# Time mix on one core: decay's low-rank product over rows and difference, key's scale on VectorE, bonus behind the first scores

## What is computed

```
h  = rms_norm(x, norm_g[0, 0])
xx = pad(h)[:-1] - h                                  # the token before, less this one
xr, xw, xk, xv, xa, xg = [h + xx * mu[i] for i in range(6)]
r, k, v = xr @ w_rkv[0], xk @ w_rkv[1], xv @ w_rkv[2]
w = -softplus(-(w_decay0 + tanh(xw @ w_decay1) @ w_decay2)) - 0.5
a = sigmoid(a0 + (xa @ a1) @ a2)
g = sigmoid(xg @ g1) @ g2
kk = k * k_k, scaled to length 1 in each head
k  = k * (1 + (a - 1) * k_a)
S_t = S_{t-1} * exp(-exp(w_t)) + (S_{t-1} @ -kk_t) (kk_t * a_t) + v_t k_t ;   y_t = S_t @ r_t
y  = group_norm(y) + sum(r * k * r_k) * v             # the last term is the bonus
out = (y * g) @ w_o
```

## Time and profile before

| | |
|---|---|
| runs, us | 1520.93 median of 3 (1519.63 to 1522.9) |
| profiled execution, us | 1519.45, with a span of 1517.7 |
| PE busy | 1413.9 us, 93% of the span |
| DVE, ACT busy | 61% and 50% |
| chain that ended last | PE 84%, DVE 9%, ACT 5%, issue 2%, DMA 1% |
| mean granted clock of PE | 0.958 |

### The profile page before, as it was taken

The page is one execution under the profiler, slowest core; times in us unless marked ns, Lnnn a source line. Parts: engine busy times, 40 slices in busy tenths (PEclk is TensorE's granted clock), DMA queues, the critical chain, the costliest instruction groups (busy, mean ns, idle before and its releaser), DMA issues.

```text
span 1517.7 us, 27277 instructions
## 1 busy us (share of the span) xinstructions
PE 1413.9 (93%) x11109; PEld 1266.0 (83%) x11109; DVE 928.3 (61%) x1355; ACT 754.1 (50%) x1166; POOL 43.9 (3%) x79
## 2 busy tenths in 40 slices
PE   5988988789999898899998999999999998899998
PEld 4867988379999787799997898799997787789997
DVE  6847332666676757666767465755557566565554
ACT  4562321165555755655557464544445464454443
POOL 5000000010000000000000000010001000000000
PEclk9998988599999999999999999999999999999999
DMA  7420001455555440555554554556654543245550
GB/s 221 135 103 1 4 3 44 166 155 193 188 172 194 142 168 25 186 203 193 167 193 147 186 185 148 164 174 191 193 187 146 178 165 102 84 159 180 190 191 29
DMA packets 135073, 222.25 MB, mean 146 GB/s; under 512 B 6137, under 2 KB 105697, under 8 KB 134720
## 3 DMA queue, kind: packets, MB, share of 16 engines
q1 hardware_dynamic: 132688, 214.19, 43.4%
q0 software_dynamic: 2144, 6.61, 1.4%
q10 hardware_dynamic: 144, 0.06, 0.0%
HBM read 219.77 MB, written 1.05 MB: 145 GB/s over the span
## 4 chain that ended last, share of the span: by engine, by line
PE 84%; DVE 9%; ACT 5%; issue 2%; DMA 1%; SPq 0%; DVEq 0%; ACTq 0%
PE ps L477 81%; DVE ulo L463 1%; ACT uhi L455 1%; DVE scratch L1799 1%; PE ps L771 1%; DVE x_sb L1773 1%; DMA raw<-in_w_rkv 1%; PE ps L1082 0%; DVE scratch L2087 0%; DVE xn_lo L1761 0%; DVE xs L1749 0%; ACT scratch L1310 0%; DVE x_sb L1779 0%; PE ps L918 0%; ACT xn_hi L1341 0%
## 5 line engine op out<-in xcount | busy, mean ns | idle before, releaser
L463 DVE TENSOR_TENSOR ulo<-raw,uhi 128x1024 fp32r<-128x1024 f32 x400 | 488.3, 1224 | 383.4 <-ACT uhi L455 383.1
L455 ACT ACTIVATE uhi<-raw 128x1024 fp32r<-128x1024 f32 x400 | 422.7, 1059 | 442.8 <-PE ps L477 437.5
L477 PE MATMUL ps<-xn_hi,uhi 128*128 128x256 f32 x1472 | 418.0, 284 | 6.7 <-DVE xn_lo L1815 2.6
L477 PE MATMUL ps<-xn_lo,uhi 128*128 128x256 f32 x1472 | 416.5, 283 | 0.0
L477 PE MATMUL ps<-xn_hi,ulo 128*128 128x256 f32 x1472 | 416.4, 283 | 0.0
L477 PEld LDWEIGHTS ps<-xn_hi,uhi 128*128 128x128 f32 x1472 | 282.3, 192 | 10.5 <-issue 4.0
L477 PEld LDWEIGHTS ps<-xn_lo,uhi 128*128 128x128 f32 x1472 | 282.4, 192 | 1.7
L477 PEld LDWEIGHTS ps<-xn_hi,ulo 128*128 128x128 f32 x1472 | 282.3, 192 | 0.0
L477 PE MATMUL ps<-uhi,xm_hi 128*128 128x512 f32 x512 | 201.3, 393 | 1.8 <-DVE xm_lo L2035 1.1
L477 PE MATMUL ps<-ulo,xm_hi 128*128 128x512 f32 x512 | 200.6, 392 | 0.0
L477 PE MATMUL ps<-uhi,xm_lo 128*128 128x512 f32 x512 | 159.9, 391 | 0.0
(11 more groups left out here) (273 smaller groups left out, 1331.2 us busy)
## 6 DMA issues: line engine op xcount, KB each, us to landing
raw<-in_mlp_w SPq DMA_DIRECT2D x64, 1024.0 KB, 5.3
raw<-in_w_up SPq DMA_DIRECT2D x44, 1024.0 KB, 5.1
raw<-in_w_down SPq DMA_DIRECT2D x22, 1024.0 KB, 4.9
raw<-in_gmlp_w_in SPq DMA_DIRECT2D x16, 1024.0 KB, 5.4
raw<-in_fox_w_in SPq DMA_DIRECT2D x16, 1024.0 KB, 5.3
raw<-in_w_rkv SPq DMA_DIRECT2D x12, 1024.0 KB, 6.2
raw<-in_gmlp_w_out SPq DMA_DIRECT2D x8, 1024.0 KB, 4.8
raw<-in_w_o_rwkv SPq DMA_DIRECT2D x4, 1024.0 KB, 5.9
```

The costliest lines, as they stand in the source:

```text
L455: nc.scalar.activation(ring_unit(uhi, m, n), raw_unit(n, j), ACT.Copy).then_inc(hi_done, 1)
L463: nc.vector.tensor_tensor(ring_unit(ulo, m, n), raw_unit(n, j), ring_unit(uhi, m, n).bitcast(F32), ALU.subtract).then_inc(lo_done, 1)
L477: return nc.tensor.matmul(o, l, r, start=start, stop=stop, skip_group_check=True)
```

## The change

- `weight_stream`: the first slot of `r` is loaded ahead of `L1A`, which becomes the second slot.
- ACT's and DVE's `upto(2)` at the start go: ACT copies `hT` first, then writes a second, scaled copy of `w_decay1` behind `L1A` (rows times `mu[1]`, 8 instructions of 64 columns), then splits units 0 and 1. DVE subtracts at once, piece by piece (`xx_done`), and splits unit 0 only after the mix for r, unit 1 in the middle of `xn_lo`.
- The decay's product is no longer over a mix: PE multiplies `w_decay1` with `hT` and the scaled copy with the difference `xx`, 8 products each into one bank, so 24 products in place of 16. `mix(1)` is gone.
- DVE's order during `r` is: unit 2, the small vectors, mix 2, unit 3, mix 5, unit 4, `xm_lo`, unit 5, mix 3, units 6 and 7. ACT rounds the mix for k after quarter 0 of `r` and not after quarter 1.
- `key_scale` moves from ACT to DVE (8 `tensor_scalar` with two per-partition scalars), behind unit 11.
- The bonus's sums stand behind the two `sb` stages and go to bank 0; ACT empties them there, behind the split of units 24 and 25.

```diff
-    phase("lora1", [("L1A",)])
-    phase("r", [u(rkv[0], 256 * q) for q in range(4)])
+    r = [u(rkv[0], 256 * q) for q in range(4)]
+    phase("r", [r[0], ("L1A",), *r[1:]])
...
-    stages = [("kn", q, 0) for q in range(4)] + [("bonus", 0, 0)] + prepare(0)
+    first = prepare(0)
+    stages = [("kn", q, 0) for q in range(4)] + first[:2] + [("bonus", 0, 0)] + first[2:]
...
# tensor
-            for j in range(2):
-                for k in range(NF):
-                    pe.wait_ge(lmix_done, NF * j + k + 1)
-                    last = mm(bank(j, T)[64 * j:64 * j + 64, :], l1a[:, 128 * k + 64 * j:128 * k + 64 * j + 64],
-                              mixes[j][:, k, :], k == 0, k == NF - 1)
-                last.then_inc(lora_ps, 1)
+            for k in range(NF):
...
+                pe.wait_ge(hT_done, k + 1)
+                mm(bank(4, T)[0:64, :], l1a[:, 128 * k:128 * k + 64], hT[:, k, 1:T + 1], k == 0, False)
+            for k in range(NF):
+                if k == 0:
+                    pe.wait_ge(lw_done, 1)
+                if k % 2 == 0:
+                    pe.wait_ge(xx_done, k // 2 + 1)
+                last = mm(bank(4, T)[0:64, :], l1a[:, 1024 + 64 * k:1088 + 64 * k], f3(S(S_X))[:, k, :], False,
+                          k == NF - 1)
+            last.then_inc(lora_ps, 1)
+            for k in range(NF):
+                pe.wait_ge(lmix_done, k + 1)
+                last = mm(bank(1, T)[64:128, :], l1a[:, 128 * k + 64:128 * k + 128], f3(S(S_MB))[:, k, :], k == 0,
+                          k == NF - 1)
+            last.then_inc(lora_ps, 1)
...
+            pe.wait_ge(lora_done, 1)
             proj("r", 0, xn_hi, xn_lo, first_split=0, split_done=rlo_done)
...
# scalar
-            upto(2)
...
+            l1a = raw[:, special[0] % RAW, :]
+            act.wait_ge(landed[special[0] % RAW], landed_at(special[0]))
+            for k in range(NF):
+                last = A_(l1a[:, 1024 + 64 * k:1088 + 64 * k], l1a[:, 128 * k:128 * k + 64], ACT.Copy,
+                          scale=col(V_MU + 8 + k))
+            last.then_inc(lw_done, 1)
+            upto(2)
...
-            proj("r", f3(S(S_R)), after={1: lambda: mixhi(1, S_MA, xm_hi)})
+            proj("r", f3(S(S_R)), after={0: lambda: mixhi(1, S_MA, xm_hi)})
...
-                 after={0: decays, 1: decays_back, 2: key_scale})
+                 after={0: decays, 1: decays_back})
...
# vector
+            dve.wait_ge(proj_done, 12)
+            for f in range(NF):
+                last = TS(f3(S(S_W))[:, f, :], f3(S(S_A))[:, f, :], col(V_KA + f), omka[:, f:f + 1], ALU.mult, ALU.add)
+            last.then_inc(ka_done, 1)
             upto(18)
```

More of the change, by code:

```diff
@@ L859, in _ @@
             d_gemm(pe, "v", xn_hi, xn_lo, before=before_v)
[L861 to L867, removed]
             pe.wait_ge(ops_done, 1)
-            pe.wait_ge(v_done, 2)
             def wait_moved(stage):
@@ L890, in core @@
                         wait_moved((r, i, g))
-                if name in ("sb", "sk"):
+                if name == "bonus":
+                    pe.wait_ge(v_done, 2)
+                    rk = f3(S(S_W))
+                    for tok in range(NT):
+                        for f in range(NF):
+                            last = mm(bank(0, 2, 16 * tok + 2 * f), rk[:, f, P * tok:P * tok + P], rks[:, f, :], True,
+                                      True)
+                elif name in ("sb", "sk"):
                     for j in range(4):
@@ L959, in core @@
                 last.then_inc(core_ps, 1)
-            for st in stages[5:]:
+            for st in stages[4:]:
                 core(*st)
@@ L1382, in _ @@
                        scale=col(V_NORM + 2 * b + f)).then_inc(hT_done, 1)
+            l1a = raw[:, special[0] % RAW, :]
[5 more added lines that the diff above has]
+            upto(2)
             act.wait_ge(lora_ps, 1)
-            A_(lh[0:64, :], bank(0, T)[0:64, :], ACT.Tanh).then_inc(lora_done, 1)
+            A_(lh[0:64, :], bank(4, T)[0:64, :], ACT.Tanh).then_inc(lora_done, 1)
             act.wait_ge(lora_ps, 2)
@@ L1422, in decays_back @@
                 act.sem_inc(ee_done, 1)
-            def key_scale():
-                act.wait_ge(proj_done, 12)
-                for f in range(NF):
-                    last = A_(f3(S(S_W))[:, f, :], f3(S(S_A))[:, f, :], ACT.Identity, scale=col(V_KA + f),
-                              bias=omka[:, f:f + 1])
-                last.then_inc(ka_done, 1)
             proj("k", f3(S(S_K)), squares=f3(S(S_H)), square_cols=V_KK,
-                 after={0: decays, 1: decays_back, 2: key_scale})
+                 after={0: decays, 1: decays_back})
             act.wait_ge(ksum_done, 1)
@@ L1438, in _ @@
                 A_(xs[:, tok, :], acc(tok), ACT.Copy).then_inc(v_done, 1)
-            act.wait_ge(core_ps, 5)
-            A_(sm[:, 16:48], bank(4, 32), ACT.Copy).then_inc(moved[0], 1)
             upto(26)
@@ L1444, in _ @@
             for k, (name, i, g) in enumerate(stages):
-                if name not in (*core_act, "rv", "tok", "u"):
+                if name not in (*core_act, "rv", "tok", "u", "bonus"):
                     continue
                 act.wait_ge(core_ps, k + 1)
+                if name == "bonus":
+                    A_(sm[:, 16:48], bank(0, 32), ACT.Copy).then_inc(bon_done, 1)
                 for q, b in enumerate(ring_bank[k]):
@@ L1794, in _ @@
                           hT[:, 2 * b:2 * b + 2, 1:T + 1], ALU.subtract)
-            step(last)
+                last.then_inc(xx_done, 1)
+            dve.wait_ge(xx_done, 4)
             def mix(k, dst, done=None):
@@ L1817, in _ @@
                 if f == 3:
-                    upto(3)
+                    upto(2)
+            upto(3)
             dve.wait_ge(vec_ps, 2)
             vectors([1, 2, 3, 4], 2)
+            mix(2, S_MA)
             upto(4)
-            dve.wait_ge(lora_ps, 1)
-            mix(2, S_MA)
-            upto(6)
-            mixlo(1, S_MA, xm_hi, xm_lo)
-            upto(7)
             dve.wait_ge(lora_ps, 2)
             mix(5, S_MB)
-            upto(8)
+            upto(5)
+            mixlo(1, S_MA, xm_hi, xm_lo)
+            upto(6)
             dve.wait_ge(mixlo_done, 1)
             mix(3, S_MA)
+            upto(8)
             dve.wait_ge(vec_done, 2)
@@ L1855, in _ @@
             dve.wait_ge(dd_done, 1)
-            TT(S(S_MB), S(S_MA), S(S_W), ALU.subtract).then_inc(dd_done, 1)
+            step(TT(S(S_MB), S(S_MA), S(S_W), ALU.subtract))
+            dve.sem_inc(dd_done, 1)
+            upto(12)
+            dve.wait_ge(proj_done, 12)
+            for f in range(NF):
+                last = TS(f3(S(S_W))[:, f, :], f3(S(S_A))[:, f, :], col(V_KA + f), omka[:, f:f + 1], ALU.mult, ALU.add)
+            last.then_inc(ka_done, 1)
             upto(18)
```

17 lines of the change are left out of this document (10 added, 7 removed).

## The result

The changed kernel took 1506.09 us (median of 4 runs, 1504.22 to 1511.5), the kernel before 1521.91 on the same chip (1519.63 to 1523.7). The ratio is 0.9906, with a 95% interval of 0.9883 to 0.993.

A forecast was written before the change was run, and what follows sets the result against it. PE's own work bounds most of the execution, so only its waits in the first 150 us can go: 4.9 + 1.9 + 1.6 = 8.4 off 1519.45, predicted median 1512.5 us (forecast 1510.5 to 1515, range 1507.5 to 1517.7).

The forecast's parts named there:

- time lost in `r`: During `r`: DVE's splits behind larger pieces lose 0.1, 1.5, 0.5 and 1.5 us, leaving 4.9 of the opening's 5.75.
- idle before `head_sums`: End of `k`: without `key_scale` on ACT, PE's idle of 4.21 us falls to 2.3, a gain of 1.9.
- wait before `ad`: End of `v`: ACT splits units 24 and 25 earlier, masks and `ad` follow, a gain of 1.6 us.
- sum at `ad`: Gains of 4.9 in opening and `r`, 1.9 at end of `k`, 1.6 at end of `v`: 8.4 us.
- The opening: Before unit 0: DVE begins `xn_lo` at 23.4 and not 29.25, PE finishes unit 0 at 28.25: gain 5.75 us.
- The key's scale: On DVE it takes 2.2 to 3.3 us, hidden by 6.07 us of DVE idle before units 13 and 14: cost 0.
- The bonus: End of `v`: its 3.63 us end at 142.8, inside PE's idle stretch before `ad` at 145.5, so covered.
- The profiled execution took 1519.45, so 1511.05: Whole kernel: 8.4 us off the profiled execution; the median lies 1.5 above it, giving 1512.5.
- PE late in the opening: Rival: `L1A` lands 2 us later and the clock falls, costing 3.2 more; together 5.2, 1517.7 us; chance 0.14.
- `L1A` last: Rival: `L1A` finishes with the other slots of `r`, near 22.6; 4.9 us slower, 1525.8; chance 0.05.
- Clock gains as well: Rival: shorter idle keeps PE's clock up, 1.7 us more at `head_sums`, up to 1.4 from `ad`: 1509.4; chance 0.15.
- The change gives nothing: Rival: splits during `r` held up by more than one mix each; four more 1.5 us stalls, 1518.5; chance 0.03.

The follow-up runs named there:

- the mix as an operand: Changed kernel with the decay's 16 products over the mix again, `mix(1)` back on DVE, no scaled weights, split order kept: 1512.37 us, ratio 0.9955 to the kernel before.
- the splits moved: Changed kernel with each of DVE's splits of units 3 to 7 during `r` ahead of the large piece before it: 1505.8 us, ratio 0.9908 to the kernel before.
- the masks first: Changed kernel with DVE's split of units 24 and 25 behind the masks of the first score stage: 1504.44 us, ratio 0.9896 to the kernel before.
- key's scale alone: Kernel before with only the key's scale moved to VectorE (DVE): 1518.73 us, ratio 0.9984.
- bonus alone: Kernel before with only the bonus moved behind the score stages: 1518.11 us, ratio 0.9985.
- opening alone: Kernel before with only load order, product over rows and difference, and split order during `r` changed: 1515.03 us, ratio 0.9968.
- changed, second: The changed kernel unaltered, compared again with the kernel before: 1510.61 us, ratio 0.9939.
- changed, `L1A` first: Changed kernel with `L1A` loaded ahead of unit 0's slot again: 1508.27 us, ratio 0.9924 to the kernel before.
- changed, third: The changed kernel unaltered, compared a third time with the kernel before: 1509.82 us, ratio 0.9921.
- the one with filler: Changed kernel with ten needless float32 products on PE in its idle stretch before `head_sums`, output unchanged: 1504.11 us, ratio 0.9887 to the kernel before.
- last quarter first: Changed kernel with ACT emptying and squaring the last quarter of `k` ahead of unit 18's high part: 1506.18 us, ratio 0.9893 to the kernel before.
- all together: Changed kernel with DVE's splits one place earlier during `r`, masks ahead of units 24 and 25, last quarter of `k` emptied first: 1499.35 us, ratio 0.9847 to before.

## Why the prediction was right in its parts and short in its sum

Up to `ad`, step by step, with the first profile of the changed kernel against the earlier trace rows:

| step | predicted | measured |
|---|---|---|
| unit 3's high part (34.00 before) | 28.25, gain 5.75 | 27.94, gain 6.06 |
| PE's waits in `r`, units 3 to 6 | 0.1, 1.5, 0.5, 1.5 | none, 1.13, 0.20, 1.18 |
| time lost in `r`, units 3 to 7 (2.9 before) | 3.7 | 51.37 - 27.94 - 7 x 2.88 = 3.3 |
| end of `r` | gain 4.9 | 56.86 - 51.20 = 5.66 |
| idle before `head_sums` | 2.3 | 2.42; its start 100.60 - 93.16 = 7.44, so 1.8 on top |
| wait before `ad` | 2.7, gain 1.6 | 1.82; 147.13 - 137.98 = 9.15, so 1.8 more than the 7.34 at the first score |
| sum at `ad` | 8.4 | 9.15 |

**The opening held.** Its mechanism is shown by the two kernels that take it apart: the mix as an operand costs 3.2, the rest are the splits. Of the gain of 6.06 some 0.4 is none of the change's: PE's transposes began at 8.18 and not at 8.63, since the first small load landed earlier. Two terms were too small. ACT's copy of 64 columns I took as 0.17 between bounds of 0.08 and 0.33; it is 2.06 / 8 = 0.26 each. The weights were ready at 15.61, PE's first eight products through at 15.50, and that cost PE 0.16, but the opening nothing: ACT had its first `xn_hi` by 22.8 and DVE only came to `xn_lo` at 23.21, so it was DVE that was last and not ACT, as I had it. There the mix was too small, 7.68 / 16 = 0.48 and not 0.447. My 0.447 was a mean over 24 mixes, and one of them is held up in either kernel. In the changed one it is this, with POOL's instruction that stands beside it:

```profile
20.29 1.20 POOL L634 TENSOR_SCALAR_AFFINE_SELECT xs<-xs 16x1024 f32<-16x1024 f32 x1
20.38 1.38 DVE L1811 SCALAR_TENSOR_TENSOR scratch<-scratch,vec 128x256 f32<-128x256 f32 x1
```

In the kernel before the same pair stands at 21.53 and 21.62, with the same durations. The other mixes take 0.47 to 0.56 and follow each other every 0.39 to 0.49. No run moved POOL's instruction, so that it is the cause is not tested; but a cost of 0.9 us that comes once doesn't shrink with the number of mixes.

**The time lost in `r` was put too high by 0.4.** It is counted from split to split on ACT: unit 3's high part to the split behind the last unit, less seven units of 2.88. Before it was 2.9, the prediction has 3.7 (1.5 + 0.5 + 1.5 + 0.1, and by a slip the 0.1 once more), and the changed kernel has 3.3: unit 3 was in time, and units 4, 5 and 6 waited less than I had. The three idle rows of PE add up to 2.5 only. In a run the passes start every 0.12 and are recorded 0.28 long, and the idle time is counted from the end of that 0.28; behind a wait the second pass starts 0.22 after the first. So each wait costs some 0.25 more than its row says. The cause is the one named: with the splits moved 0.3 is left of the 3.3.

**The key's scale was hidden**, as predicted. It took 2.67 / 8 = 0.33 each, between the bounds of 0.27 and 0.41 and not at the lower one, and DVE still idles 4.63 us behind it:

```profile
72.13 2.67 DVE L1873 TENSOR_SCALAR scratch<-scratch,vec,sm 128x256 f32<-128x256 f32 x8
74.72 1.21 DVE L467 TENSOR_TENSOR ulo<-raw,uhi 128x1024 fp32r<-128x1024 f32 x1
80.56 2.36 DVE L467 TENSOR_TENSOR ulo<-raw,uhi 128x1024 fp32r<-128x1024 f32 x2 [4.63 <-ACT uhi L459]
```

**The bonus was covered**, and what was late next were units 24 and 25, as the step says; the kernel with the masks first shows it.

**Where the sum failed: "The profiled execution took 1519.45, so 1511.05".** That step carries the 8.4 from `ad` to the end, as if all behind it took the same time. It doesn't, from one execution to the next. The table has the start of `ad`, the first instruction of the group norm behind the recurrence (a DVE reduction), the time between them, and from there to the end of the span; the code behind `ad` is the same in all of them.

| profile of | `ad` | group norm | between | from there on |
|---|---|---|---|---|
| before | 147.13 | 273.51 | 126.4 | 1244.2 |
| key's scale alone | 147.67 | 274.17 | 126.5 | 1242.7 |
| bonus alone | 146.52 | 272.52 | 126.0 | 1243.8 |
| opening alone | 141.66 | 268.25 | 126.6 | 1241.7 |
| changed, first | 137.98 | 259.32 | 121.3 | 1243.2 |
| changed, second | 138.24 | 260.64 | 122.4 | 1242.5 |
| changed, `L1A` first | 139.77 | 263.32 | 123.5 | 1243.3 |
| changed, third | 139.71 | 265.77 | 126.1 | 1242.8 |

In the first comparison 5.0 of the 15.2 us of span lie between `ad` and the group norm, and 1.0 behind that. The 126.1 of the third profile and the 121.3 of the first belong to the same kernel, so they can be laid side by side. Ninety us behind `ad`, at the same products, PE's timeline reads, first profile and then third:

```profile
225.75 7.57 PE L481 MATMUL ps<-raw 64*64 64x64 f32 x252 [0.29 <-issue]
```

```profile
229.99 10.19 PE L481 MATMUL ps<-raw 64*64 64x64 f32 x295 [2.09 <-issue]
```

and the stretches of 3 us around them, first profile and then third:

```profile
226.00:229.00 3.00, 3.00 (x110) 3.00 (x106) 0.76 (x2) 0.98 (x2) 0.00 (x0) 1.00 0.12 45
229.00:232.00 3.00, 3.00 (x110) 3.00 (x108) 0.00 (x0) 2.22 (x5) 0.00 (x0) 1.00 0.03 5
```

```profile
228.00:231.00 3.00, 1.01 (x19) 1.00 (x20) 1.21 (x2) 0.00 (x0) 0.00 (x0) 0.78 0.16 60
231.00:234.00 3.00, 3.00 (x76) 3.00 (x74) 0.00 (x0) 0.60 (x1) 0.00 (x0) 0.65 0.02 5
```

PE stands for 2.09 us and waits for nothing that the profile shows, and the clock falls behind it, to 0.65 over a stretch, so that 3 us of it hold 76 products and not 110. The profiles of before, of the opening, the key's scale and the bonus alone have this stop too (1.92, 2.33, 2.20 and 2.87 us); the first and second of the changed kernel and the one with `L1A` first have at most 0.44 us of it. From the place of the stop to the group norm the third profile takes 37.9 us and the first 33.9, so stop and clock are 4.0 of the 4.7 between them. Before it was 35.9: against the first profile 2.0 of the 5.0 lie there, and the other 3.0 ahead of the stop, where the clock differs as well (0.50 from 195 to 201 before, 0.72 from 186 to 192 in the first profile, both 48 us behind `ad`).

The stop happens while three loads of 512 KB on POOL's queue fill the DMA engines. An instruction block moves among them. These are the us in which it starts, of the first profile (223 to 224) and then of the third (227 to 228), with queue and kind, packets, MB, share of the 16 DMA engines:

```profile
q0 software_dynamic: 73, 0.26, 82.9%
q8 instruction: 1, 0.02, 6.0%
```

```profile
q0 software_dynamic: 101, 0.37, 96.8%
q8 instruction: 1, 0.02, 6.0%
```

I read the stop as PE's instructions coming late behind the loads. Thirteen of the fourteen profiles have idle time of this kind at this point, from 0.20 to 3.72 us, and they bear the reading out in two ways. First the place: in twelve of them, whatever the kernel, 3114 to 3116 passes of PE since the start of the program precede it, and in the one with filler 3242, 127 more; in the first profile two more such rows, of 0.44 and 0.19 us, stand 252 and 378 passes behind the first. So it hangs on how many instructions PE has had, and not on what they compute or on the time. Then the block: in the 20 us ahead blocks of `q8` follow each other every 3.4 to 4.6 us. Across the loads the gap is 6.0 to 6.4 us in the five profiles without the stop and 7.9 to 9.3 in the nine with it, and in all thirteen PE goes on 2.2 to 2.4 us after the block began to move (third profile: 227.81 and 229.99; first: 223.47 and 225.75). That the loads are what delays the block is not tested: no run moved them, and the profile doesn't say whose block it is. The Trainium skill (Runtime: NRT & Kernel Launch, Instruction fetch mechanics) says that fetching is hidden because an engine issues more slowly than its memory is filled; if the reading is right, this trace disagrees, with 2.09 us.

Whether the change makes the stop rarer stays open. Of the profiles above all four with an old opening, key's scale or bonus have it, and of four of the changed path one has it. But four of the six variants built on the changed kernel have it: with splits moved and with filler it is 0.44 and 0.35 us, with the mix as an operand, masks first, last quarter first and all together 2.79, 2.36, 2.36 and 3.72. A second source of scatter is the clock in `v`. The first and third profile begin its third unit at 106.13 and 106.22, PE is busy from there to the end of `v` in both, and `ad` still begins 1.7 apart.

Nor is it shown that what exceeds the landmark is scatter alone. In all thirteen comparisons the medians differ by more than the starts of `ad` do, by 0.5 us at the least and 8.8 at the most; that is why most of the gains stated beforehand were too low. The one profile of the kernel before has a part in that, since its execution was faster than the median of its runs by 0.3 to 3.9 us; whether it is all, one profile can't tell.

So the forecast of 8.4 was low by 0.75 in its own terms (0.3 in the opening, 0.4 in `r`, the rest at `v` and `ad`); what is left, 2.8 us of the mean of 12 and 6.6 of the first comparison's 15.8, is no step of it. The range had no room for that: it was made of the costs of the edits alone, and the same kernel's executions go from 1504.2 to 1514.6.

**The rivals.** PE late in the opening, and `L1A` last: neither occurred; PE had 0.16 us of idle time in its 48 passes and a clock of 1.00 from 10 to 24. Clock gains as well: not at `head_sums`, where 2.42 us of idle time still brought 0.50, and not at `ad`, where the clock was low too:

```profile
134.00:140.00 6.00, 4.14 (x46) 3.89 (x46) 5.93 (x14) 0.21 (x2) 0.00 (x0) 0.56 0.00 1
```

The mechanism is real, as the two kernels at `head_sums` show (1.7 us, the amount worked out), but the change doesn't get to the point from which it pays. The change gives nothing: no; its condition, stalls in `r` behind more than one mix each, didn't occur.

## What to carry to other kernels

On an engine that works in order, put a short step that another engine is waiting for ahead of a long one that only must be done some time; moving five unit splits was worth about as much here (3.0 us at the end of `r`) as leaving out eight mixes (3.2). When a wait is removed, look up who is late next, since that decides the gain: 4.04 us of work taken off ACT gave 1.8. And a change in the first tenth of a program shifts all behind it against its transfers; before a few us are put down to the edit, split the execution at a landmark behind the edit, compare both sides, and look at more than one execution. A mean over instructions hides a delay that comes once (here 0.9 us in one mix of 24), so look at the single rows before scaling it.

## What the runs showed of the hardware that I had not expected

- PE stopped for 1.9 to 3.7 us without a wait that the profile shows, in nine of the fourteen profiles and always behind the same number of its instructions; it went on 2.2 to 2.4 us after an instruction block began to move. From `ad` to the group norm the nine took 126.0 us in the mean, the five others 122.1.
- The granted clock fell to 0.50 behind 2.42 us of idle time before `head_sums` and stayed at 1.00 there behind 1.42, but in the opening it also stayed at 1.00 behind the 3.24 us that the mix as an operand brought at 12 to 15 us, and in the changed kernel it fell from 1.00 to 0.50 at 134 to 136 us, in the bonus, while PE was busy. The length of the idle time alone doesn't say what the clock will do; what does is open.
- The clock in `v` differs between executions with PE busy all the time: in the stretch from 116 to 122 it was 0.86 in the first profile and 0.63 in the third.
- A 1 MB slot at the start of the program landed at 11.8 to 14.1 us in executions with the same loads ahead of it.
- ScalarE's copy of 64 columns costs 0.26 us, where 256 columns cost 0.33: three quarters of the price for a quarter of the size.
- One DVE mix in the opening took 1.38 us where its neighbours took 0.47, in step with a POOL instruction of 1.20 us, in both kernels.
